# A decoder trunk on eight cores: the first token group's projection in four steps of four chunks

## The reference, cut to what matters

```python
def _layer(x, ...):                       # x (batch, L, 2048), two layers
    z = x @ w_in                          # (B, L, 3584): q, k, v, conv gates, pooling input
    q, k, v, gb, gc, h, pin = jnp.split(z, idx, -1)
    a = _swa_prompt(q, k, v, ...)         # sliding-window attention, 16 q heads, 4 kv heads
    c = gb * _dwconv3(u_ext, conv_w)      # short gated convolution
    pm = _pool_mix(p_ext, ...)            # multi-scale pooling
    mix = jnp.concatenate([a, c, pm], -1) @ w_o
    x = _ln(DEEPNORM_ALPHA * x + mix, ln1_g, ln1_b)
    hc = _dwconv3(jnp.concatenate([ffn_prev, x @ w_up], 1), ffn_conv_w)
    g, val = jnp.split(hc, 2, -1)
    f = (jax.nn.silu(g) * val) @ w_down
    x = _ln(DEEPNORM_ALPHA * x + f, ln2_g, ln2_b)
```

## Time and profile before

| | us |
|---|---|
| median of 3 runs (lowest, highest) | 2840.01 (2839.45, 2842.6) |
| profiled execution, its own time | 2839.04 |
| its span, slowest core (core 2) | 2837.5 |
| spans of the eight cores | 2828.8 to 2837.5 |
| TensorE busy on core 2 | 2729.5 (96%) |
| first matmul on core 2 | 11.80 |

### The profile page before, as it was taken

How to read it: one execution, slowest core, us unless ns; L and a number is a source line. 1 busy time by engine, 2 the same in 40 slices (tenths; PEclk the granted TensorE clock), 3 DMA queues, 4 the chain that set the end, 5 groups by cost and what they waited for, 6 DMA issues and landing times.

```text
span 2837.5 us, 52754 instructions; the slowest of 8 cores (2828.8 to 2837.5 us)
## 1 busy us (share of the span) xinstructions
PE 2729.5 (96%) x18484; PEld 1739.9 (61%) x18484; DVE 1476.1 (52%) x3278; ACT 931.4 (33%) x2005; POOL 496.2 (17%) x755
## 2 busy tenths in 40 slices
PE   7999999999999999999999989999999999999994
PEld 4655666666666666665665556566666666666653
DVE  0375466563555355445616644775535544563546
ACT  1565055330232033113636630643203311330236
POOL 2221063000000000001623102610000000000024
PEclk9999999999999999999999999999999999999997
DMA  9515524434444443443472154344454344434425
GB/s 163 104 31 157 109 49 79 81 77 80 76 74 69 82 75 69 67 89 62 106 192 42 37 157 94 60 75 75 80 88 75 69 68 85 73 61 82 75 46 125
DMA packets 84349, 238.12 MB, mean 84 GB/s; under 512 B 9288, under 2 KB 30032, under 8 KB 83536
## 3 DMA queue, kind: packets, MB, share of 16 engines
q0 software_dynamic: 61136, 190.23, 38.6%
q1 hardware_dynamic: 22944, 44.41, 5.1%
HBM read 405.99 MB, written 21.27 MB: 151 GB/s over the span
## 4 chain that ended last, share of the span: by engine, by line
PE 93%; DVE 2%; ACT 2%; issue 1%; DMA 1%; POOL 1%; DVEq 0%; POOLq 0%; ACTq 0%
PE ps L196 93%; DVE xT L196 1%; DMA X<-xg 1%; ACT xT L196 1%; DVE scr L196 1%; ACT scr L196 0%; POOL xT L196 0%; ACT rstd L196 0%; DMA slab<-w_in 0%; DVE H L196 0%; POOL H L196 0%; DVE rstd L196 0%; ACT ps L196 0%; DVE small L196 0%; DVEq L191 0%
## 5 line engine op out<-in xcount | busy, mean ns | idle before, releaser
L196 PE MATMUL ps<-X,slab 128*128 128x386 bf16 (+3 forms) x10944 | 1681.7, 315 | 21.8 <-DMA slab<-w_in 11.8
L196 PEld LDWEIGHTS ps<-X,slab 128*128 128x128 bf16 x10944 | 1059.4, 97 | 628.1 <-issue 52.2
L196 PE MATMUL ps<-H,slab 128*128 128x384 bf16 (+1 forms) x5760 | 895.5, 314 | 0.0
L196 DVE SCALAR_TENSOR_TENSOR scr<-ps,fcw_s,scr 128x384 f32<-128x384 f32 (+1 forms) x1056 | 616.0, 584 | 410.7 <-ACT scr L196 353.9
L196 PEld LDWEIGHTS ps<-H,slab 128*128 128x128 bf16 x5760 | 561.6, 98 | 307.8 <-issue 7.1
L196 ACT ACTIVATE scr<-ps,fcw_s 128x384 f32<-128x384 f32 (+1 forms) x528 | 291.1, 553 | 1054.9 <-PE ps L196 1054.7
L196 DVE TENSOR_TENSOR xT<-xT,ps 128x384 f32<-128x384 f32 (+1 forms) x549 | 264.5, 521 | 207.8 <-PE ps L196 189.9
L196 POOL DMA_DIRECT2D slab<-w_up x176 | 93.6, 532 | 924.7 <-PE ps L196 924.7
L196 DVE TENSOR_TENSOR H<-scr 128x384 bf16<-128x384 f32 (+3 forms) x278 | 143.4, 518 | 98.1 <-ACT scr L196 69.6
L196 ACT ACTIVATE scr<-xT 128x384 bf16<-128x384 f32 (+1 forms) x192 | 94.5, 496 | 226.0 <-DVE xT L196 181.9
L196 DVE SCALAR_TENSOR_TENSOR xT<-xT,lna_s,ps 128x384 f32<-128x384 f32 x144 | 83.8, 583 | 139.6 <-PE ps L196 139.6
(11 more groups left out here) (111 smaller groups left out, 858.5 us busy)
## 6 DMA issues: line engine op xcount, KB each, us to landing
slab<-w_up POOLq DMA_DIRECT2D x176, 512.0 KB, 6.6
slab<-w_dn POOLq DMA_DIRECT2D x96, 384.0 KB, 5.7
slab<-w_in POOLq DMA_DIRECT2D x56, 512.0 KB, 10.6
slab<-w_o POOLq DMA_DIRECT2D x32, 512.0 KB, 7.5
xT<-xr SPq DMA_DIRECT2D x16, 531.0 KB, 7.4
xT<-spill SPq DMA_DIRECT2D x16, 531.0 KB, 9.1
slab<-w_dl POOLq DMA_DIRECT2D x16, 512.0 KB, 6.6
spill<-xT SPq DMA_DIRECT2D x2, 3072.0 KB
```

Of the source, the lines that this page charges most:

```text
L196: bi = getattr(engobj, name)(*a_, **k_)
```

## The change

The first two slabs are loaded in quarters of four chunks (128 x 1024 elements, 256 KB). POOL issues, for each q of 0 to 3: chunks 4q to 4q+3 of X's group 0, quarter q of slab 0, quarter q of slab 1. For group 0 of layer 0 the four output tiles take their four PSUM banks at once and are accumulated side by side: four matmuls of each tile, then the next four of each, in four steps; the four evictions are recorded behind the last step. All other loads, groups and layers are as they were. Slabs in two parts now name two quarters per part, which gives the same waits.

```diff
+    def load_part(self, i, h):
+        key, parts, nc_ = self.plan[i]
+        t = self.tiles[i % NSLOT]
+        st = 4096 // len(parts)
+        ap, nk = parts[h]
+        self.P.dma("pool", lambda e: e.dma_start(out=t[:, h * st:h * st + nk * nc_], in_=ap),
+                   writes=[("slab", i % NSLOT, r) for r in range(h * st // 1024, (h + 1) * st // 1024)])
...
         def lhs(k, m):
-            o = (k // half) * 2048 + (k % half) * nc_ + m * 128
-            return t[:, o:o + 128], ("slab", i % NSLOT, k // half)
+            o = (k // half) * st + (k % half) * nc_ + m * 128
+            return t[:, o:o + 128], ("slab", i % NSLOT, o // 1024)
...
-                    SM.plan.append((("in", l, i), wi(i), 256))
+                    if l == 0 and i < 2:
+                        SM.plan.append((("in", l, i), [(w_in[l, i, q // 2, :, 1024 * (q % 2):1024 * (q % 2) + 1024], 4) for q in range(4)], 256))
+                    else:
+                        SM.plan.append((("in", l, i), wi(i), 256))
...
-            for c in range(0, 16, 4):
-                load_x(0, c, c + 4)
-                if c == 0:
-                    SM.load_next()
-            SM.load_next()
+            for q in range(4):
+                load_x(0, 4 * q, 4 * q + 4)
+                SM.load_part(0, q)
+                SM.load_part(1, q)
+            SM.loaded = 2
             load_x(1, 0, 8)
...
+                    if l == 0 and gi == 0:
+                        pss = [ps_next() for _ in range(4)]
+                        for q in range(4):
+                            for t, (ps, psr) in enumerate(pss):
+                                for k in range(4 * q, 4 * q + 4):
+                                    lap, lres = qs[t // 2](k, t % 2)
+                                    rap, rres = rhsX(k, lo, hi)
+                                    P.pe(lambda e, ps=ps, lap=lap, rap=rap, k=k, n=hi - lo: e.matmul(
+                                        ps[:, 0:n], lhsT=lap, rhs=rap, start=(k == 0), stop=(k == 15)), reads=[lres] + rres, writes=[psr])
+                        for t, (ps, psr) in enumerate(pss):
+                            evict_q(t, ps, psr, lo, hi)
+                        continue
```

More of the change, by code:

```diff
@@ L250, in load_next @@
         self.loaded += 1
-        key, parts, nc_ = self.plan[i]
-        t = self.tiles[i % NSLOT]
-        for h, (ap, nk) in enumerate(parts):
-            self.P.dma("pool", lambda e, t=t, ap=ap, h=h, nk=nk: e.dma_start(out=t[:, h * 2048:h * 2048 + nk * nc_], in_=ap),
-                       writes=[("slab", i % NSLOT, h)])
+        for h in range(len(self.plan[i][1])):
+            self.load_part(i, h)
     def get(self, key):
@@ L264, in get @@
         half = parts[0][1]
+        st = 4096 // len(parts)
         def lhs(k, m):
-            o = (k // half) * 2048 + (k % half) * nc_ + m * 128
-            return t[:, o:o + 128], ("slab", i % NSLOT, k // half)
+            o = (k // half) * st + (k % half) * nc_ + m * 128
+            return t[:, o:o + 128], ("slab", i % NSLOT, o // 1024)
         def full(k):
-            o = (k // half) * 2048 + (k % half) * nc_
-            return t[:, o:o + nc_], ("slab", i % NSLOT, k // half)
+            o = (k // half) * st + (k % half) * nc_
+            return t[:, o:o + nc_], ("slab", i % NSLOT, o // 1024)
         lhs.full = full
```

## The result

| | before | after |
|---|---|---|
| median of 21 runs each, us | 2840.71 | 2846.19 |
| ratio of the runs compared | | 1.0018, 95% interval [1.001, 1.0026] |
| profiled execution, its own time | 2839.04 | 2846.19 |
| span of its slowest core | 2837.5 (core 2) | 2844.6 (core 0) |
| mean span of the even cores in it | 2836.05 | 2843.07 |

The change costs 5 us, and the interval lies wholly above 1. The forecast was 2839.5, its range ended at 2845.2. It missed in size, and no change was forecast where there is a loss. The **ratio** has an interval. The **mean** is that of the same runs less that of the kernel before on the same chip, in us, with a standard error of 0.4 to 0.7 (larger ones are given).

The account below looks back on a forecast made before the run. The prediction took the start to be bound by bytes, TensorE waiting for X's group 1. Landing 0, issues and banks 0, clock -0.5 against 2839.04 gave 2838.5, or 2839.5 on the median's scale; range 2836.3 to 2845.2.

Parts of the forecast that it names:

- What bounds the start: Start on TensorE: bytes bound it; the unbroken stretch begins at 37.14 us, when the second half of X's group 1 lands.
- The second rival: Group 0 on TensorE: its earlier end reaches the end of the kernel, 2.2 us faster, 2837.8; chance 0.03.
- The landing term: Load line ahead of X's group 1: same bytes and pace per KB, so its second half still lands at 37.0; 0 us.
- The bounds of -1.2 to +5.9 us: Slab quarters' transfers: from the best pace of a row to each taking as long as 384 KB of X.
- The forecast's own test: X's group 1: forecast wrong if its second half lands over 3 us earlier or later, or TensorE doesn't wait for it.
- The first rival: Slab quarters between 9.2 and 27.1 us: small transfers cost more each, +5.9 us (2846) to +11.4 (2851); chance 0.09.
- The clock term: TensorE around group 1: longer idle time moves the clock's fall into 8 matmuls where it costs nothing; -0.5 us.
- The issues: POOL at the start: four more issues at 0.53 us each, on an engine that waits anyway; 0 us.
- the banks: PSUM after group 0: evictions run from about 26.5 to 30, before group 1 needs a bank at 32.55; 0 us.
- the eight-place rule: POOL waits for the transfer eight places earlier; the line stays filled. Rival that it starves: chance 0.02.
- The matmuls' schedule: Group 0 on TensorE: four bursts ending at 28.7 against 30.95, idle time before group 1 growing from 1.60 to about 3.9 us.

Follow-up runs that it names:

- e3: Kernel before with the change's four-step matmuls of group 0, loads as before; ratio 0.9995, mean -1.2 us.
- j2: The change with contiguous quarters, X in contiguous blocks and sorted waits (latest recorded last); ratio 0.9992, mean -2.9 us.
- h2: Kernel before with X in contiguous blocks and sorted waits (latest recorded last); ratio 0.9988, mean -2.7 us.
- e1: The change with its quarters read from a copy where each is one contiguous block; ratio 1.001, mean +3.3 us.
- g2: The change with 28 extra memsets, restoring the order of waits of before at nearly all places; ratio 1.0016, mean +4.2 us.
- h4: The change with its quarters read as 4 KB out of rows padded to 6 KB; ratio 1.0016, mean +4.3 us.
- g3: The change with contiguous quarters and 28 extra memsets that nearly restore the order of waits of before; ratio 1.0006, mean +1.6 us.
- g1: Kernel before with four extra memsets, giving the change's order of waits on ACT; ratio 1.0007, mean +1.6 us.
- h3: Kernel before with its waits reversed, on the latest recorded instruction first; ratio 1.0011, mean +2.7 us.
- j1: The change with contiguous quarters, 28 extra memsets and the matmuls of before; ratio 1.0002, mean +0.5 us.
- e2: The change's loads with the tile-by-tile matmuls of before; ratio 1.0012, mean +3.5 us.

## Why the prediction was wrong

**What bounds the start: right.** TensorE waits for X's second half, before and after, on all four even cores (the wait ahead of it was put down to an eviction on cores 0 and 6 before, 0.78 and 0.70 us, which the prediction's cores did not show, and it bounds nothing); e3 moved TensorE's work by ten microseconds at no cost, and j2 against h2 shows that the early end of group 0 reaches nothing. The second rival, a gain of 2.2 us, is out.

**The landing term: wrong, and this is the first failed step.** "I take 0, since three sizes show no rise per KB as the transfer gets smaller." The argument on size held: e1, same sizes, starts 0.2 us late. But I compared transfers by their KB alone, and the change altered a second thing, which stands in the diff: the source `w_in[..., 1024 * (q % 2):...]` takes half of each 8 KB row. All slab rows of the trace before were whole rows, and X's rows (24 KB apart, of which 6 to 12 KB are read) have another step; none bounded a 4 KB read at a step of 8 KB. It measured 3.1 us on the even cores' start in after's execution (0.8 in g2's, where the odd cores paid), 3.4 to 3.8 us on the sum of the even and odd marks in both, and 1.8 us of the time by after against e1 (0.8 by h4, 2.6 by g2 against g3). The bounds of -1.2 to +5.9 us held it, the value taken did not. The forecast's own test, second half more than 3 us late, was met: 41.2 against 37.0.

**The first rival** named the right place and nearly the right time (2846), for another reason than that which acted. "It decides once a quarter takes over 2.1 us": three of the eight did, with 2.39, 3.04 and 2.89. A rival that is priced by size is not confirmed by a time that fits; e1 and h4 separate the two.

**The terms that I did not have.** "All other loads, groups and layers are as they were" is what the change's text says, and the sum rests on it. It isn't so. Every later instruction kept its work and its dependences, but not the order of its waits. This is the second failed step. It is worth 0.9 to 1.7 us (g1, g3 against e1, g2 against after), no single one of them beyond doubt, and another order costs 2.7 (h3, interval above 1).

**The clock term: wrong sign.** I gave -0.5 us for a fall of the clock that would come where it costs nothing. Core 2's 216 matmuls took 33.36 us again, and the mean of the even cores rose from 32.85 to 33.53, so 0.7 us was lost there. Core 0 had its fall in the 8 matmuls, as core 4 before, and still took 34.24 for the 216. Over the whole program the even cores lost granted clock (0.9884 to 0.9859), and by the table of dates they are 3 to 4 us later behind 1370, a place that the prediction takes as unchanged.

**The issues, the banks, the eight-place rule: right.** POOL was never late: X's group 1 was issued at 16.62 and 19.66 (forecast 16.0 and 17.5) and landed at about 37.6 and 41.2. No matmul waited for a bank.

**The matmuls' schedule: wrong in its numbers, without effect.** Group 0 ended at 36.2 instead of 28.7, idle time before group 1 was 1.50 instead of 3.9, both because the last quarters came 5 us later than counted.

**The sum.** +1.8 (8 KB step) + 1.7 (order of waits) + 1.6 (what is left in g3) = 5.1, by after to e1 to g3 to before. Each term has a standard error of 0.4 to 0.7, and the last is not told from zero by its ratio (1.0006 [0.9997, 1.0016]).

**What stays open.** First, those 1.6 us: j1 (+0.5) and g3 (+1.6) differ only in the order of the matmuls, which in e3 alone cost nothing, and with standard errors of 0.7 and 0.4 the two can be the same. Second, why a step of 8 KB is slow, and whether the array's place in HBM has a part in it. Cores 1 and 3 begin to load between 12 and 16 us, just ahead of the slow microseconds, which fits 1.3 us for early quarters and 3.0 for later ones (the very first took 2.39); no run had the even cores alone. Third, why the even and the odd cores share the cost so differently (marks +3.0 / +0.8 in after, +0.6 / +2.9 in g2, with one set of loads and matmuls). Fourth, the way from the order of waits to the time: the stop near 1371 grew in all kernels with after's order, but the clock fell behind it on 6 of 28 cores only, and on none in g1 and h3.

## What to carry to other kernels

When a transfer is cut in two, look at what happens to its source's rows as well as at its size: half of each row at a step of 8 KB moved the sum of the even and odd marks by 3.4 to 3.8 us, the same bytes in blocks of their own by 0.3 to 0.9. When an edit adds or removes recorded instructions, compare the lists of waits far behind it before calling the rest unchanged; an order that hangs on numbering should be fixed (sorted) before changes of 0.1% are judged. And a stage that waits for bytes is shortened by no order of its matmuls.

## What the runs showed of the hardware

- 4 KB reads per partition at a step of 8 KB moved 106 to 131 GB/s on core 2 over 6 us, where whole rows moved 158 to 199 and the same quarters without a step 147 to 152, at a DMA busy share of 1.0 to 1.3 in all these rows. A step of 6 KB was as good as none (marks' sum 116.5 and 116.1, against 119.6).
- The order in which an instruction waits for its two or three semaphores is worth microseconds over a program of 2840: the two orders latest last (-1.6, its ratio's interval includes 1) and latest first (+2.7, its interval above 1) are 4.3 us apart.
- A stop of TensorE of 2.21 us was followed by granted clocks of 0.51 and 0.64 on core 0 of e1 and by 1.00 on core 0 of g1. The clock fell on 6 of 28 even cores behind a stop of 2.21 us at this place, and on none of 36 behind one of 2.09 us.
- Transfer time that is lost can be paid by the cores that run the other program: with the same loads the mark moved by +3.0 / +0.8 us (even / odd) in after and by +0.6 / +2.9 in e2 and g2.
